# The first RMS norm of a transformer block: squares summed on TensorE, constant multiplies in its rests, one pair of weight columns loaded earlier

## What is computed

```python
def rmsnorm(x, g):
    xf = x.astype(jnp.float32)
    y = xf * lax.rsqrt(jnp.mean(xf * xf, axis=-1, keepdims=True) + RMS_EPS)
    return (y * g.astype(jnp.float32)).astype(x.dtype)

def modulate(h, shift, scale):
    return h * (1.0 + scale[:, None, :]) + shift[:, None, :]

cs = jax.nn.silu(c)
mod = cs @ ada_w[l] + ada_b[l]
shift1, scale1, gate1, shift2, scale2, gate2 = jnp.split(mod, N_MOD, axis=-1)
h = modulate(rmsnorm(x, norm1_g[l]), shift1, scale1)
proj = h @ w_in[l]
qa, ka, va, qb, kb, vb, ga, gb = jnp.split(proj, offsets, axis=-1)
```

## Time and profile before

| what | us |
|---|---|
| three runs | 1810.68, 1810.7, 1811.23 |
| median | 1810.7 |
| the profiled execution | 1811.6 |
| its span, first to last instruction | 1809.8 |
| PE busy | 1790.5 (99%) |
| DVE busy | 959.0 (53%) |
| ACT busy | 725.4 (40%) |

### The profile page before, as it was taken

One profiled execution on the slowest core, in us unless ns is written; L12 is line 12 of the kernel. 1 busy time (PEld: TensorE's weight loads), 2 busy tenths in 40 slices (PEclk: granted clock), 3 DMA queues, 4 the chain that ended last, 5 costly groups with the idle time before them and its releaser, 6 DMA issues.

```text
span 1809.8 us, 20638 instructions
## 1 busy us (share of the span) xinstructions
PE 1790.5 (99%) x8372; PEld 1468.5 (81%) x8372; DVE 959.0 (53%) x1396; ACT 725.4 (40%) x1124; POOL 19.5 (1%) x47
## 2 busy tenths in 40 slices
PE   6999999999999999999999999999999999999999
PEld 4787788888888888887888888887878888888887
DVE  8487646763434356677553434345746554434343
ACT  4455532442323244476342323244456442323231
POOL 0100000000000000000000000000000000000000
PEclk9999999999999999999999999999999999999999
DMA  8465454232223223212222323232221223232322
GB/s 330 127 194 196 164 165 138 87 112 93 95 93 104 94 93 130 92 47 70 94 93 93 105 93 98 91 102 86 89 82 58 86 89 106 93 105 94 102 93 73
DMA packets 55040, 196.77 MB, mean 109 GB/s; under 512 B 6417, under 2 KB 6929, under 8 KB 54946
## 3 DMA queue, kind: packets, MB, share of 16 engines
q1 hardware_dynamic: 52272, 187.72, 30.9%
q0 software_dynamic: 2384, 7.51, 1.5%
q10 hardware_dynamic: 290, 0.22, 0.0%
HBM read 193.28 MB, written 2.14 MB: 108 GB/s over the span
## 4 chain that ended last, share of the span: by engine, by line
PE 99%; DVE 1%; DMA 0%; ACT 0%; SPq 0%; issue 0%; DVEq 0%
PE ps L356 28%; PE ps L358 28%; PE ps L357 28%; PE ps L407 2%; PE ps L409 2%; PE ps L408 2%; PE ps L863 1%; PE ps L506 1%; PE ps L752 1%; PE ps L797 1%; PE ps L587 1%; PE ps L783 0%; PE ps L561 0%; PE ps L846 0%; DMA XT<-in_X 0%; PE ps L717 0%
## 5 line engine op out<-in xcount | busy, mean ns | idle before, releaser
L356 PE MATMUL ps<-R0h,WH 128*128 128x512 f32 x1248 | 491.8, 394 | 3.5 <-DVE R0l L1554 3.5
L358 PE MATMUL ps<-R0h,WL 128*128 128x512 f32 x1248 | 486.8, 390 | 0.0
L357 PE MATMUL ps<-R0l,WH 128*128 128x512 f32 x1248 | 486.4, 390 | 0.0
L994 ACT ACTIVATE WH<-RAW 128x1024 fp32r<-128x1024 f32 x298 | 314.2, 1055 | 405.4 <-PE ps L358 359.4
L1497 DVE TENSOR_TENSOR WL<-RAW,WH 128x1024 fp32r<-128x1024 f32 x298 | 364.2, 1223 | 192.1 <-ACT WH L994 187.9
L356 PE MATMUL ps<-R1h,WH 128*128 128x512 f32 x976 | 380.4, 390 | 0.0
L358 PE MATMUL ps<-R1h,WL 128*128 128x512 f32 x976 | 379.7, 389 | 0.0
L357 PE MATMUL ps<-R1l,WH 128*128 128x512 f32 x976 | 379.7, 389 | 0.0
L356 PEld LDWEIGHTS ps<-R0h,WH 128*128 128x128 f32 x1248 | 234.9, 188 | 55.9 <-DVE R0l L1554 3.9
L358 PEld LDWEIGHTS ps<-R0h,WL 128*128 128x128 f32 x1248 | 234.7, 188 | 49.4
L357 PEld LDWEIGHTS ps<-R0l,WH 128*128 128x128 f32 x1248 | 234.9, 188 | 48.2 <-issue 0.7
(11 more groups left out here) (299 smaller groups left out, 1298.9 us busy)
## 6 DMA issues: line engine op xcount, KB each, us to landing
RAW<-in_W SPq DMA_DIRECT2D x338, 512.0 KB, 3.3
ARENA<-in_W SPq DMA_DIRECT2D x12, 512.0 KB, 10.2
XT<-in_X SPq DMA_DIRECT2D x4, 512.0 KB, 8.8
ARENA<-bias_scratch POOLq DMA_DIRECT2D x8, 256.0 KB, 4.4
XT<-in_X POOLq DMA_DIRECT2D x8, 256.0 KB, 3.6
out_x<-XT SPq DMA_DIRECT2D x7, 256.0 KB, 2.0
ARENA<-bias_scratch POOLq DMA_DIRECT2D x8, 128.0 KB, 3.7
ARENA<-in_SGW POOLq DMA_DIRECT2D x1, 512.0 KB, 4.5
```

The lines of the kernel that those rows point to most:

```text
L356: e.matmul(ps(b), wh, hi, start=first, stop=False)
L357: e.matmul(ps(b), wh, lo, start=False, stop=False)
L358: return e.matmul(ps(b), wl, hi, start=False, stop=last)
L994: e.activation(slot(n)[0], src, ACT.Copy).then_inc(sem["w_hi"])
```

## The change

Line numbers below L457 are the same in both; further down those of the changed kernel are higher (L1504 becomes L1525, L1564 L1585, L1497 L1518, L1549 L1570, L1554 L1575, L994 L1012).

- The two columns of tile 1 are issued before qa0 and qa1.
- DVE adds only tiles 1 to 4 to tile 0. PE takes the sums of tile 5, of the added tiles 0 to 4, of tile 6 and of tile 7 in four calls of `token_sums`, accumulated in the same columns of PSUM.
- ACT takes the root straight from PSUM with scale 1/1024 and epsilon as bias; `mean_eps` is gone. Its table is loaded after the second silu, by a root of one column that waits for the constants (`d_con`).
- `keep_busy` on PE multiplies the identity by 256 constant columns (128 once) into bank 5, which is written anew later: 5 times after the constants have landed, once after each of DVE's first three adds, once short after the sums, 3 times after the spread, once after `scaled(0)`.
- DVE makes the two dot products of tile 1 before the reciprocal. The `lo` of qa0 and of qa1, which stood before it, stand behind `scaled(0)` and behind `scaled(1)`; on ACT `hi` of the two goes behind the root. In the step k = 3 the extra `ada` stands behind `shifted_rest`.

```diff
-    plan = columns(0) + FIRST[:2] + columns(1) + FIRST[2:] + columns(2, 3, 4, 5, 6) + [("vb", 0)] + columns(7)
+    plan = columns(0) + columns(1) + FIRST + columns(2, 3, 4, 5, 6) + [("vb", 0)] + columns(7)
...
+            def keep_busy(times, n=256):
+                for _ in range(times):
+                    e.matmul(ps(5, 0, n), ident, con[:, 0:n], start=True, stop=True)
+
             def norm_start():
                 e.wait_ge(sem["d_con"], 16)
+                keep_busy(5)
+                for k in range(1, 4):
+                    e.wait_ge(sem["ssq"], k)
+                    keep_busy(1)
+                e.wait_ge(sem["sq"], 6)
+                token_sums(xs[:, 5, :], 0, True, False)
                 e.wait_ge(sem["ssq"], 7)
-                token_sums(xs[:, 0, :], 0).then_inc(sem["ss"])
+                token_sums(xs[:, 0, :], 0, False, False)
+                e.wait_ge(sem["sq"], 7)
+                token_sums(xs[:, 6, :], 0, False, False)
+                e.wait_ge(sem["sq"], 8)
+                token_sums(xs[:, 7, :], 0, False, True).then_inc(sem["ss"])
+                keep_busy(1, 128)
                 e.wait_ge(sem["rs"], RS[0] + 2)
                 spread(nrs, 7, "spr")
                 free[7] = (("nrm0", 8),)
+                keep_busy(3)
+                e.wait_ge(sem["nrm0"], 1)
+                keep_busy(1)
...
+                e.wait_ge(sem["d_con"], 16)
+                e.activation(NS[:, 6, 0:1], ones1, ACT.Sqrt)
                 gain(0)
...
-                hi(2)
-                sqrt(nrs, RS[0] + 1)
-                hi(1)
+                e.wait_ge(sem["ss"], 1)
+                e.activation(nrs, PSB[6][:, 0:4], ACT.Sqrt, scale=1.0 / 1024, bias=pc("eps")).then_inc(sem["sqrt"])
                 gain(1)
                 for k in range(KT):
-                    if k > 1:
+                    if k < 2:
+                        hi()
+                    else:
                         gain(k)
...
                     if k == 1:
-                        hi(3)
+                        hi(4)
...
-                for k in range(1, KT):
+                for k in range(1, 5):
                     e.wait_ge(sem["sq"], k + 1)
                     if k > 1:
                         e.wait_ge(sem["ssq"], k - 1)
-                    e.tensor_tensor(xs[:, 0, :], xs[:, 0, :], xs[:, k, :], ALU.add).then_inc(sem["ssq"])
-                lo(2)
-                mean_eps(0, nrs)
-                rsqrt(0, nrs)
+                    e.tensor_tensor(xs[:, 0, :], xs[:, 0, :], xs[:, k, :],
+                                    ALU.add).then_inc(sem["ssq"], 4 if k == 4 else 1)
                 scale_shift(1)
+                e.wait_ge(sem["sqrt"], 1)
+                e.reciprocal(nrs, nrs).then_inc(sem["rs"], 2)
                 e.wait_ge(sem["spr"], 1)
                 scaled(0)
+                lo(1)
+                shifted_rest(0)
                 scaled(1)
-                shifted_rest(0)
+                lo(1)
                 shifted_rest(1)
                 lo(3)
...
-                    elif k < 7:
+                    elif 3 < k < 7:
                         ada()
                     shifted_rest(k)
+                    if k == 3:
+                        ada()
```

## The result

The change makes the kernel slower: median 1818.9 us (five runs, 1816.91 to 1819.36) against 1810.7, ratio 1.004 with a 95% interval of 1.0029 to 1.0052. The forecast was 1813.3. The profiled execution took 1817.5 us, its span is 1815.7 (before: 1811.6 and 1809.8). Measured twice more, with 5 and 8 runs, the same kernel had medians 6.9 and 5.4 us over the kernel before beside it, so 8.2 is the highest of three; counted run by run, the median of all 18 is 6.9 over.

The account below looks back on a forecast made before the run. DVE's feed, not PE's start, was taken as the near bound. A dry queue makes k = 2's rest 2.4 us late and PE waits 0.7 at k = 4; k = 7 at 56.5 against 53.91 gives +2.6, 1813.3 us (range 1810.9 to 1815.6).

Parts of the forecast that it names:

- part 5: PE's first projections: k = 2 starts at 35.3, PE waits 0.7 us at k = 4, k = 7 starts at 56.5 (before 53.91).
- part 4: Moved lo delay ka and va; the DMA queue runs dry, DVE waits 1.9 us for tile 2's columns, k = 2's rest 2.4 late.
- part 1: Sums on PE with constant multiplies: four token_sums take 3.2 us, sums there at 18.1, reciprocal at 18.5 as before.
- what can be won with DVE as it is: At k = 7, DVE's last rest is ready at 51.75, PE wants it at 53.91: no more than 2.1 us.
- My last rival: TensorE's clock rises late or constant multiplies don't raise it, so the sums come late: +7.5, 1818.2 us; chance 0.10.
- Parts 2 and 3: DVE: tile 1's dot products before the reciprocal, until 18.1; then scaled(0) at 19.4, three lo from 24.4 to 27.8, 0.5 later.
- the rival that came true: TensorE falls to the lower rate in the gap ahead of va, costing 1.9 us: +3.9, 1814.6 us; chance 0.14.

Follow-up runs that it names:

- b2: Kernel before plus seven constant multiplies ahead of the sums of squares and seven behind the spread: 1810.7 us beside 1811.3, ratio 0.9999.
- d2: Changed kernel with sums back on DVE, tile 2's columns ahead of ka and va, both splits earlier, old order at k = 3: 1811.1 us beside 1811.3.
- a1: Changed kernel with the two columns of tile 2 issued ahead of ka and va: 1815.0 us, ratio 1.002.
- c1: Changed kernel with the splits of qa0 and qa1 brought back towards their old time, on ACT hi of qa0 ahead of the root: 1813.7 us, ratio 1.0014.
- a2: Changed kernel with ten more constant multiplies on PE in the gap between tiles ka and va: 1815.7 us, ratio 1.0024.
- d1: Changed kernel with the sums of squares back on DVE, seven adds and one call of token_sums: 1816.5 us, ratio 1.0028.
- b1: Kernel before with only the lo of qa0 and qa1 moved behind scaled(0) and scaled(1): 1817.0 us, ratio 1.0034.

## Why the prediction was wrong

**The steps that failed.** The chain, a dry queue, then a DVE that waits, then a PE that waits, was right, and it is the larger part of the loss. The step that failed is in part 5: the forecast let TensorE keep its full rate across the gap ahead of va. The clock fell there and cost 1.9 us. Beside it two terms were too small: the landings behind the dry queue (part 4, 1.0 us) and the sums (part 1), whose price at the full rate didn't hold in all runs.

**The bound was read rightly, but too wide.** PE has no margin from the first projections on; the constant difference of 1755.9 us shows it. The forecast put what can be won with DVE as it is at 2.1 us, from k = 7. The 0.4 us at k = 3 is the bound, since PE needs its full 4.08 us for each k behind it: b2 used that margin up to 0.09 us, d2 to 0.3, and their medians are 0.5 and 0.2 us under the kernel before, neither clear of noise.

**Part 1, the sums.** Forecast 18.5 for the reciprocal, seen 18.77, 18.52 and 18.30: right in the profiles. But the forecast took one price of `token_sums` at the full rate for all four, 3.2 us, from a row with wide multiplies just ahead. They took 3.63 us in the three profiles, with the clock falling just behind them, and 4.2 and 4.8 in a1 and c1, where it fell before they were done. My last rival named the clock and the sums, but as a clock that rises late or never, with 7.5 us and a chance of 0.10. A mild form of it, some 1.7 us, would be most of what sets the upper nine of the 18 runs apart; no profile shows it in the change itself.

**Parts 2 and 3.** The dot products ended at 17.3 rather than 18.1, `scaled(0)` came at 19.7 (forecast 19.4), the three splits started at 24.6 (24.4). The last two are right within 0.3 us.

**Part 4, the dry queue.** The mechanism is as forecast, with the wait in the place named; its size was too small in this profile. The columns landed at 31.05 instead of 29.6 and DVE waited 2.9 us instead of 1.9. The times from issue to landing, of ka, va and the first column of tile 2, and of the latter's second:

```profile
DMA to landing us min/median/max: 3.2/3.2/3.2
DMA to landing us min/median/max: 3.8/3.8/3.8
DMA to landing us min/median/max: 4.7/4.7/4.7
DMA to landing us min/median/max: 6.1/6.1/6.1
```

The lone transfer took the 3.2 of the earlier trace rows. Of the three that follow, va took 0.5 more than I gave it and the two columns landed 1.2 and 1.9 us apart instead of 1.3: the rate was 371, 350 and 365 GB/s in the stretches from 26 to 32 us, and 420 from 32 on. In the two later profiles DVE waited 2.1 and 2.2 us, close to the forecast. The Trainium skill, "DMA: Bandwidth & Descriptors", Specifications, with its 358 GB/s as the limit from HBM for one core, would have been nearer for these few us; the steady stretches, with 401 to 424 GB/s from 32 to 44 us, are above it.

**Part 5, and the rival that came true.** I counted 0.7 us of waiting at k = 4 and no fall of the clock. The gap ahead of va was 5.0 us (forecast 4.1), the clock fell in it, and 12 multiplies ran at the lower rate. At the full rate va would have ended by 36.9, k = 4 would have waited for its rest (44.81, ready 45.6) and k = 7 started at 57.85; it started at 59.75. So of the 5.8 us in the profile 2.6 are as forecast, 1.3 the later rests of DVE (landings and reciprocal), 1.9 the clock. a2 confirms the last number (1.9 to 2.2). I gave this rival 0.14, because no row showed a fall after a gap. In the seven profiles of this study with a gap of 2.0 to 5.0 us ahead of va and nothing in it (2.0, 2.7, 3.8, 4.1, 4.2, 4.4, 5.0) the clock fell in it or just behind it; in c1, with 1.6 us, it stayed up. That agrees in kind with the Trainium skill, "TensorE: Matmul & The Clock Gate", Part 1, by which the clock is at half after idle time and only sustained work brings it back, and I should have given it more weight than the absence of a row.

**The median.** The other 2.3 us between the profile's 5.9 and the medians' 8.2: the profiled execution of before lies 0.9 over its median, that of the change 1.4 under its own. The profile is of the lower group, and three of the first five runs are of the upper, so part of the 8.2 is the luck of five runs: the other two medians are 6.9 and 5.4 over. All three lie above the forecast's range, which ends 4.9 over.

## What to carry to other kernels

When an operation is moved later, ask which transfers wait for the buffer that it frees, and what stands behind those on the same in-order queue: here two splits that cost nothing in their own chain dried the queue for 3 us. An engine that runs without a wait may still be fed by one with a margin of 0.4 us; then its own earlier start is worth no more than that margin. And work that is moved to TensorE has the price of the clock it finds: four calls of `token_sums` took 3.63, 4.2, 4.8 or 6.96 us.

## What the runs showed of the hardware

- TensorE's clock fell while the engine worked without a pause from 9.3 us on, in the third of four blocks of one-column fp32 multiplies (c1: 32 records, 4.82 us instead of 3.63). In the change's own three profiles it fell after the sums, at 19.0 to 20.1 us, so most of the constants there ran at the lower rate. In d1 it fell at about 17.0 us, after a pause of 1.07 us and one call of `token_sums`.
- It also fell around a gap of 2.0 us (a1), not at once: the first five multiplies behind the gap were fast, the next slow, for 3.0 us. In the change's first profile it was down for 5.2 us behind the gap of 5.0 us.
- After a pause of the DMA queue the first transfers were slower than the steady ones: 350 to 371 GB/s from 26 to 32 us in the change against 420 later, 365 and 375 from 26 to 30 us in b1.
- The column of the granted clock reads 1.00 at the start of a profile also where the spacing of the multiplies shows the lower rate: 0.427 us from 23.32 to 27.3 us in the kernel before and, with gaps between, from 22.69 to 29.3 us in b1, where it reads 1.00 until 36 us. Up to the first change that it shows, the spacing has to be read instead.
